# Half of the router's gates added into a DRAM table by indirect DMAs, the other half built by one-hot products at half the density

## Time and profile before

| | |
|---|---|
| runs | 4674.74, 4667.36, 4668.51 us; median 4668.51 |
| span of the profiled execution | 4667.2 us; what lies around the span is not given for it |
| TensorE | 4455.6 us busy, 95% of the span |
| VectorE, ScalarE, GpSimd | 54%, 31%, 7% |
| mean granted clock | 0.981 of 2.4 GHz |
| HBM | 444.94 MB read, 73.40 MB written, 111 GB/s |

### The profile page before, as it was taken

How to read it: one execution, slowest core, us unless ns; L and a number is a source line. 1 busy time by engine, 2 the same in 40 slices (tenths; PEclk the granted TensorE clock), 3 DMA queues, 4 the chain that set the end, 5 groups by cost and what they waited for, 6 DMA issues and landing times. The chain is left out here.

```text
span 4667.2 us, 58760 instructions
## 1 busy us (share of the span) xinstructions
PE 4455.6 (95%) x22068; PEld 3726.6 (80%) x22068; DVE 2500.4 (54%) x3598; ACT 1454.4 (31%) x1579; POOL 306.1 (7%) x178
## 2 busy tenths in 40 slices
PE   8999889999999999989998999899999999999997
PEld 7888658888887778878996887777778888888886
DVE  4333444334335743346777343478888884555554
ACT  3222443222223532223443122233333332222221
POOL 0000000000000000001111000000000001333331
PEclk9999989999999999989999999999999999999998
DMA  3232102223322133222211232345545566565553
GB/s 118 96 90 85 37 29 88 99 88 101 99 89 73 28 91 99 84 72 64 63 59 52 85 98 85 115 131 138 137 128 176 180 193 216 189 198 191 191 193 108
DMA packets 514507, 519.84 MB, mean 111 GB/s; under 512 B 41173, under 2 KB 475469, under 8 KB 513374
## 3 DMA queue, kind: packets, MB, share of 16 engines
q1 hardware_dynamic: 514398, 518.41, 36.4%
HBM read 444.94 MB, written 73.40 MB: 111 GB/s over the span
## 5 line engine op out<-in xcount | busy, mean ns | idle before, releaser
L78 DVE TENSOR_TENSOR w_lo<-w_raw,w_hi 128x2048 fp32r<-128x2048 f32 (+2 forms) x326 | 667.8, 2050 | 919.4 <-ACT w_hi L72 919.3
L72 ACT CAST w_hi<-w_raw 128x2048 fp32r<-128x2048 f32 (+2 forms) x326 | 557.6, 1713 | 1259.1 <-PE psum L3119 491.5
L94 PE MATMUL psum<-h_hi,w_hi 128*128 128x512 f32 x1552 | 612.5, 395 | 16.3 <-DVE w_lo L78 13.3
L96 PE MATMUL psum<-h_hi,w_lo 128*128 128x512 f32 x1552 | 607.6, 391 | 0.0
L95 PE MATMUL psum<-h_lo,w_hi 128*128 128x512 f32 x1552 | 607.5, 391 | 0.0
L94 PE MATMUL psum<-h_hi_peer,w_hi 128*128 128x512 f32 x1104 | 437.6, 396 | 23.9 <-DVE w_lo L2966 16.1
L96 PE MATMUL psum<-h_hi_peer,w_lo 128*128 128x512 f32 x1104 | 431.2, 391 | 0.0
L95 PE MATMUL psum<-h_lo_peer,w_hi 128*128 128x512 f32 x1104 | 430.8, 390 | 0.0
L3117 PE MATMUL psum<-pr_act_hi,w_hi 128*128 128x512 f32 x1024 | 398.3, 389 | 0.0
L3118 PE MATMUL psum<-pr_act_lo,w_hi 128*128 128x512 f32 x1024 | 398.3, 389 | 0.0
L3119 PE MATMUL psum<-pr_act_hi,w_lo 128*128 128x512 f32 x1024 | 398.3, 389 | 0.0
(11 more groups left out here) (467 smaller groups left out, 7432.2 us busy)
## 6 DMA issues: line engine op xcount, KB each, us to landing
w_raw<-in_ffn_w_gate_up_dram SPq DMA_DIRECT2D x176, 512.0 KB, 4.2
w_raw<-in_peer_u_dram SPq DMA_DIRECT2D x256, 256.0 KB, 5.1
w_raw<-in_peer_v_dram SPq DMA_DIRECT2D x128, 512.0 KB, 4.2
w_raw<-in_w_in_dram SPq DMA_DIRECT2D x64, 512.0 KB, 4.3
peer_hidden<-pr_q SPq DMA_DIRECT2D x64, 512.0 KB, 4.0
peer_gates<-pr_staged SPq DMA_DIRECT2D x8, 4096.0 KB, 12.9
pr_back<-peer_hidden SPq DMA_DIRECT2D x64, 512.0 KB, 6.2
pr_gate<-peer_gates SPq DMA_DIRECT2D x64, 512.0 KB, 7.2
```

The source lines that it names most:

```text
L72: c.nc.scalar.copy(c.hi[:, slot, :cols], c.raw[:, slot, :cols]).then_inc(c.hi_ready, 1)
L78: c.nc.vector.tensor_tensor(c.lo[:, slot, :cols], c.raw[:, slot, :cols], c.hi[:, slot, :cols].bitcast(F32), ALU.subtract).then_inc(c.lo_re ...
L94: c.nc.tensor.matmul(out, w_hi, x_hi, start=(n == 0), stop=False)
L96: mm = c.nc.tensor.matmul(out, w_lo, x_hi, start=False, stop=(n == last))
```

## The change

The 512 tokens are split. For tokens 0 to 255 (`ADDED` = 2 blocks of 128) the gates go to a table in DRAM, `gates_added`, with one element for each expert and token, 16.8 MB. The table is cleared in the stick-breaking block by 16 DMAs of 1 MB from a tile of zeros, four behind each group's loads. In `finish`, DVE now also works out where each of the 16 x 2 weights of a token belongs: three more operations, whose result goes to `place`. POOL then issues 32 indirect DMAs a head. Each takes one slot of one block, 128 weights, one from each partition, and adds them in DRAM at the 128 places. Before the next head's DMAs POOL waits until those of the last have landed. SP's first fetch waits for all 256.

For tokens 256 to 511 the one-hot way stays: 64 quads in the same 24 units, 2, 3 and 3 a unit, and four stores of 4 MB. Six transposes of `rows` in place of 12, and copies of half the width. `rows` and `place` now live through the whole layer.

In the output stage `fetch` has three DMAs in place of two (the halves of the gates come from the two tables), POOL's product is two instructions, one for each half of the tokens, and `gated` counts two a unit. The setup makes two more constants on POOL, and PE's first transpose waits for them.

```diff
@@ setup
+            pool.memset(c.zeros[:, :], 0.0).then_inc(made, 1)
+            pool.iota(c.token[:, :], pattern=[[P, 2 * TC]], base=0, channel_multiplier=1,
+                      allow_small_or_imprecise_dtypes=True).then_inc(made, 1)
...
-            pe.wait_ge(made, 13)
+            pe.wait_ge(made, 15)
@@ sb_attention
+GATE_CLEARS = 16
+        cleared = c.gates.rearrange("a p t -> (a p t)").rearrange("(n p x u) -> n p x u", n=GATE_CLEARS, p=P, u=P)
...
                 for j in range(2):
                     load_tile(c, sp, uq + i, j, wide_parts(c, j, w_in, i * 256 + j * D))
+                for q in range(GATE_CLEARS // SB_GROUPS):
+                    part = cleared[bass.ds(i * (GATE_CLEARS // SB_GROUPS) + q, 1)].rearrange("n p x u -> p (n x) u")
+                    sp.dma_start(part, c.zeros[:, :].unsqueeze(1).broadcast_to(list(part.shape))
+                                 ).then_inc(c.gates_cleared, 16)
             following(sp)
+            sp.wait_ge(c.gates_cleared, ROWS_LOADED + 16 * GATE_CLEARS)
@@ peer
+ADDED = 2
+SPREAD = TC - ADDED
-N_TG = T // TG
+N_TG = SPREAD * P // TG
+PICKS = ADDED * TOP
...
-SPREAD_ROUNDS, ROUND_UNITS = 4, 6
+SPREAD_ROUNDS, ROUND_UNITS = 2, 12
-QUADS = ((2, 3), (2, 3), (3, 3)) * 2
+QUADS = ((1, 1), (1, 2), (1, 2)) * 4
...
-                sp.wait_ge(gated, m + 1)
+                sp.wait_ge(gated, m * 2 + 2)
...
+                sp.dma_start(gate_added[:, j], c.gates[bass.ds(m * 2, 2)].rearrange("a p t -> p a t")
+                             ).then_inc(gate_loaded[j], 16)
...
                         sp.wait_ge(written[p], 16 * SPREAD_ROUNDS * ROUND_GROUPS // 2 + 16)
+                    sp.wait_ge(scattered, 16 * NH * PICKS)
...
-            pool.sem_inc(gated, 2)
+            pool.wait_ge(c.gates_cleared, ROWS_LOADED + 16 * GATE_CLEARS)
+            for n in range(NH):
+                pool.wait_ge(placed, n + 1)
+                if n:
+                    pool.wait_ge(scattered, 16 * n * PICKS)
+                for t in range(ADDED):
+                    for k in range(n * TOP, (n + 1) * TOP):
+                        pool.indirect_dma_start(
+                            out=table, out_offset=bass.IndirectOffsetOnAxis(ap=place[:, t, k:k + 1], axis=0),
+                            in_=rows[:, 2, t, k:k + 1], in_offset=None, compute_op=ALU.add).then_inc(scattered, 16)
+            pool.sem_inc(gated, 4)
...
-                    pool.tensor_tensor(prod[:, j].rearrange("p a (g t) -> p a g t", g=N_TG),
-                                       back[:, j].rearrange("p a (g t) -> p a g t", g=N_TG),
+                    some, rest_of = slice(0, ADDED * P), slice(ADDED * P, T)
+                    pool.tensor_tensor(prod[:, j, :, some], back[:, j, :, some], gate_added[:, j], ALU.mult
+                                       ).then_inc(gated, 1)
+                    pool.tensor_tensor(prod[:, j, :, rest_of].rearrange("p a (g t) -> p a g t", g=N_TG),
+                                       back[:, j, :, rest_of].rearrange("p a (g t) -> p a g t", g=N_TG),
                                        gate[:, j].rearrange("p g a t -> p a g t"), ALU.mult).then_inc(gated, 1)
...
+                step(V.scalar_tensor_tensor(spot[:, :, :], rows[:, 0, 0:ADDED, of_head], float(KEYS),
+                                            rows[:, 1, 0:ADDED, of_head], ALU.mult, ALU.add))
+                step(V.scalar_tensor_tensor(spot[:, :, :], spot[:, :, :], float(ADDED * P),
+                                            c.token[:, 0:ADDED].unsqueeze(2).broadcast_to([P, ADDED, TOP]), ALU.mult, ALU.add))
+                V.tensor_copy(place[:, :, of_head], spot[:, :, :]).then_inc(placed, 1)
...
-                for t in range(TC):
-                    mm = nc.tensor.transpose(ps[:, 6 + r % 2, t * P:(t + 1) * P], rows[:, r, t, :], c.ident[:, :])
+                for t in range(SPREAD):
+                    mm = nc.tensor.transpose(ps[:, 6 + r % 2, t * P:(t + 1) * P], rows[:, r, ADDED + t, :],
+                                             c.ident[:, :])
```

More of the change, by code:

```diff
@@ L175, in setup @@
         loaded = c.rows_loaded = [sem(c, f"rows_loaded{t}") for t in range(TC)]
+        c.gates_cleared = c.rows_loaded[3]
         ps = c.psum
@@ L2544 @@
 ROWS_LOADED = 16
+KEYS_LOADED = 16 * (NH // 2)
 BAND = 32
@@ L2584, in peer @@
         q = sb("q", [P, 2, 2, T])
-        chosen = sb("chosen", [P, 3, T])
+        chosen = sb("chosen", [P, 3, SPREAD * P])
+        rows = sb("rows", [P, 3, TC, SLOTS])
+        place = sb("place", [P, ADDED, SLOTS], U32)
         with ExitStack() as pre_ph:
@@ L2604, in peer @@
             total = sb("total", [P, 8], on=pre_ph)
-            rows = sb("rows", [P, 3, TC, SLOTS], on=pre_ph)
+            spot = sb("spot", [P, ADDED, TOP], on=pre_ph)
         with ExitStack() as spread_ph:
@@ L2612, in peer @@
         back = sb("back", [P, 2, 2, T])
+        gate_added = sb("gate_added", [P, 2, 2, ADDED * P])
         gate = sb("gate", [P, 2, N_TG, 2, TG])
         prod = sb("prod", [P, 2, 2, T])
-        keys_loaded, stored, written, hid_loaded, gate_loaded = (
-            [sem(c, f"pr_{n}{j}") for j in range(2)] for n in (
-                "keys_loaded", "stored", "written", "hid_loaded", "gate_loaded"))
+        keys_loaded, stored, written, hid_loaded = (
+            [sem(c, f"pr_{n}{j}") for j in range(2)] for n in ("keys_loaded", "stored", "written", "hid_loaded"))
+        gate_loaded = keys_loaded
         h_free = sem(c, "pr_h_free")
@@ L2620, in peer @@
         (q_taken, keys_turned, keys_taken, scored, s_taken, indexed, steps, shifted, weighed, rows_turned,
-         chosen_taken, turned, gelued, built, spread, taken, gated, hi_done, lo_done, added) = (
+         chosen_taken, turned, gelued, built, spread, taken, gated, hi_done, lo_done, added, placed, scattered) = (
              sem(c, f"pr_{n}") for n in (
@@ L2624, in peer @@
                  "shifted", "weighed", "rows_turned", "chosen_taken", "turned", "gelued", "built", "spread", "taken",
-                 "gated", "hi_done", "lo_done", "added"))
+                 "gated", "hi_done", "lo_done", "added", "placed", "scattered"))
+        table = c.gates.rearrange("a p t -> (a p t)").unsqueeze(1)
         ps = c.psum
@@ L2774, in take_chosen @@
                 act.wait_ge(rows_turned, r + 1)
-                nc.scalar.copy(chosen[:, r, :], ps[:, 6 + r % 2, :]).then_inc(chosen_taken, 1)
+                nc.scalar.copy(chosen[:, r, :], ps[:, 6 + r % 2, 0:SPREAD * P]).then_inc(chosen_taken, 1)
             def stage(o, quads):
@@ L2788, in high @@
             def high(m, j):
-                act.wait_ge(gated, m + 3)
+                act.wait_ge(gated, m * 2 + 6)
                 nc.scalar.copy(act_hi[:, j], prod[:, j]).then_inc(hi_done, 1)
@@ L2845, in _ @@
                     pool.wait_ge(hid_loaded[j], i * 16 + 16)
-                    pool.wait_ge(gate_loaded[j], i * 16 + 16)
+                    pool.wait_ge(gate_loaded[j], i * 32 + (KEYS_LOADED + 32))
                     pool.wait_ge(lo_done, m + 1)
-                    pool.tensor_tensor(prod[:, j].rearrange("p a (g t) -> p a g t", g=N_TG),
-                                       back[:, j].rearrange("p a (g t) -> p a g t", g=N_TG),
+                    some, rest_of = slice(0, ADDED * P), slice(ADDED * P, T)
[3 more added lines that the diff above has]
+                                       back[:, j, :, rest_of].rearrange("p a (g t) -> p a g t", g=N_TG),
                                        gate[:, j].rearrange("p g a t -> p a g t"), ALU.mult).then_inc(gated, 1)
@@ L2899, in finish @@
                 step(V.reciprocal(total[:, 0:TC], total[:, 0:TC]))
-                step(V.tensor_tensor(rows[:, 2, :, n * TOP:(n + 1) * TOP], weight[:, :, :],
+                of_head = slice(n * TOP, (n + 1) * TOP)
+                step(V.tensor_tensor(rows[:, 2, :, of_head], weight[:, :, :],
                                      total[:, 0:TC].unsqueeze(2).broadcast_to([P, TC, TOP]), ALU.mult))
+                step(V.scalar_tensor_tensor(spot[:, :, :], rows[:, 0, 0:ADDED, of_head], float(KEYS),
[3 more added lines that the diff above has]
+                V.tensor_copy(place[:, :, of_head], spot[:, :, :]).then_inc(placed, 1)
             def bests(half, src):
@@ L3188, in count_of_steps @@
 def count_of_steps():
-    a_head = 5 + 1 + 2 + 3 + 3 + 3 + 3
+    a_head = 5 + 1 + 2 + 3 + 3 + 3 + 3 + 2
     return NH * a_head
@@ L3343, in build @@
         c.iota = sb("iota", [P, P])
+        c.zeros = sb("zeros", [P, P])
+        c.token = sb("token", [P, 2 * TC])
         c.vec = sb("vec", [P, P])
@@ L3349, in build @@
         c.begun = sem(c, "begun")
+        c.gates = nc.dram_tensor("gates_added", [KEYS, P, ADDED * P], F32).ap()
         c.hi_ready, c.lo_ready, c.tile_used = (sem(c, n) for n in ("hi_ready", "lo_ready", "tile_used"))
```

## The result

The changed kernel takes 4696.57 us (median of 4 runs, 4695.94 to 4700.19) against 4669.35 for the kernel before (4 runs, 4667.36 to 4674.74). The ratio is 1.006, with a 95% interval of 1.0046 to 1.0074: slower by 27 us, where 4613 was predicted. The profiled execution took 4700.19, with a span of 4698.4.

A forecast was written before the change was run, and what follows sets the result against it. PE, busy for 95% of the span, was taken as the bound. −62 − 0.8 + 4.5 + 1 + 2 = −55.3 from the span of 4667.2 gave 4611.9, so 4613 with 1.3 around the span; range 4603 to 4655, chance 0.8.

The forecast's parts named there:

- Clears, setup, output stage: nothing: Stick-breaking block, setup constants and output stage: clears, two constants, split products and extra fetch are covered, costing 0 us.
- rival A: SP's wait before the first fetch: POOL's scatters come late, gain gone at 3.2 us a DMA; near 4748 at 3.5; chance 0.13.
- rival B: Search stage: POOL's instructions hold DVE up where PE waits for it; +32 us at 0.6 each, near 4645; chance 0.17.
- rival C: Spread stage: builds or copies set the pace, so PE's saving is not had; about 4655 us; chance 0.03.
- The quads, −62: Spread stage: 64 of 128 quads leave PE at 0.953 us each; −61.0 by pace, held 57 to 64, taken as 62.
- The six transposes: Turning of `rows` on PE for two blocks of tokens instead of four: six fewer transposes save 0.8 us.
- DVE's three steps, +4.5: Search stage, in `finish`: two multiply-adds and a cast at 0.25 us each, 0.75 a head, six heads; 0 to 6.
- 5 to 8: Sign to look for: the search stage longer by 5 to 8 us, with the stall after a `finish` about 1.9.
- The adds, 1.5 us each: POOL's 256 indirect DMAs: 1.5 us each, drains about 2 each, ending before 3600, so the chain costs nothing.
- rival A's last paragraph: DVE's fast one-input copies block POOL's descriptors: 3.1 us a DMA, 256 make 794 us, some 20 past the deadline.
- the deadline of 777: From the first head's readiness at 3070.5 to SP's first fetch at 3847: 777 us for POOL's DMAs and drains.
- Contention, +3: Search stage: 1 us for tiny packets on the DMA engines, 2 us for POOL holding DVE up (bounds 0 to 35).

The follow-up runs named there:

- experiment 1: The kernel before with the two new tiles, `zeros` and `token` (544 bytes), allocated at the same place but unused: 4754.96 us, ratio 1.0185.
- experiment 3: The kernel before with the tile `rows` 32 bytes longer, all later tiles 32 bytes further: 4756.02 us, ratio 1.0185.
- experiment 5: The changed kernel with `rows` shortened by 32 bytes, so later tiles move by 512 bytes and not 544: 4611.51 us, ratio 0.9881.
- experiment 2: The changed kernel with `zeros` and `token` taken out of the unused lead, so they push no other tile: 4609.26 us, ratio 0.9875 to the kernel before.
- experiment 12: experiment 2 with three blocks of tokens added instead of two (384 indirect DMAs, 32 quads): 4652.76 us, ratio 0.9967 to the kernel before.
- experiment 11: experiment 2 without POOL's 256 indirect DMAs, those tokens' gates staying zero: 4608.19 us, ratio 0.9872 to the kernel before.

## Why the prediction was wrong

**The step that failed** is the one that opens "Clears, setup, output stage: nothing", in its sentence on the setup: "Two more small constants on POOL precede PE's first transpose, but PE waits for x until 8.24 anyway". I priced the two constants by the time that it takes to fill them, and that is nothing indeed. I didn't price the space that they take. `token`, 32 bytes a partition, cost 87 us (experiments 1, 3 and 5), more than the whole change could win. None of my rivals, A, B or C, has it.

What spoke for it was in sight. The groups by form had 512-column matmuls at 389 to 391 ns and those on `mix_h`, of the same shape, at 396 to 399. `build` has a tile `lead` that nothing uses and a `rows` of 512 − 2 × `TC` numbers, an odd size for rows. I had read neither as a question of speed.

From the step, about 14,700 matmuls of 512 columns that were at the lower level × 0.0067 would be 98 us. Measured were 87. In experiment 3 PE is busy for 4547.0 us, 91.4 more than before, and idle for 207.8 instead of 211.6: a slower PE waits 3.8 us less for others. The remaining 7 us stay open; perhaps not all of the 14,700 run back to back.

**The other steps** are held against experiment 2, which has the work of the change and the distances of before. It was 4609.3 where the sum gave 4613.

- *The quads, −62: right.* The pace gave 61.0, and I took one more. The 24th spread unit's GELU is at 3810.68 and the first quad at 3489.9: 320.8 us, where 321 was named. That is 383.1 − 320.8 = 62.3 less. A quad left over costs (320.8 − 261.1) / 64 = 0.933 us. DVE and the copies didn't pace the stage (rival C): PE was busy in 319.75 of 321 us, and DVE in 213.24. The six transposes that are left cost 0.7 less than the twelve, where 0.8 was named.
- *The products of the quads are still what was read:* 512 records, as predicted.

```profile
L3144 PE MATMUL psum<-pr_first,pr_second 128*128 128x128 f32 x512 | 65.0, 275 | 4.2 <-DVE pr_first L3022 2.9 <-issue 1.3
```

- *DVE's three steps, +4.5: somewhat too high.* The two multiply-adds take 0.19 us each and the cast 0.30, and they start 0.23 us apart. The order of time around one `finish`, and PE's start behind it:

```profile
3238.09 0.19 DVE L2938 SCALAR_TENSOR_TENSOR pr_spot<-pr_rows 128x32 f32<-128x32 f32 x1
3238.32 0.19 DVE L2940 SCALAR_TENSOR_TENSOR pr_spot<-pr_spot,token 128x32 f32<-128x32 f32 x1
3238.55 0.30 DVE L2942 CAST pr_place<-pr_spot 128x32 uint32<-128x32 f32 x1
...
3241.39 2.34 DVE L3007 TENSOR_TENSOR w_lo<-w_raw,w_hi 128x1024 fp32r<-128x1024 f32 x2
...
3243.86 0.49 PE L94 MATMUL psum<-h_hi_peer,w_hi 128*128 128x512 f32 x1 [1.69 <-DVE w_lo L3007]
```

  The stall went from 1.14 to 1.69, where 1.9 was named: five such are +2.8, and a sixth, at the start of the stage, went from 0.92 to 1.25. Over the whole search stage PE is busy 348.37 of 368 us instead of 351.46, 3.1 less. The prediction named 5 to 8 as its sign.
- *The adds, 1.5 us each: too low, and it didn't matter.* One takes 1.54 us in the median and there are 0.3 between two, so the pace is 1.85. But 62 of the 256 take longer than 1.7, up to 4.45, and within a head the mean distance of two is 2.0 to 2.4. The waits for the landings of a head's adds were priced at 2 us each and took 5.0, 35.2 over seven:

```profile
L2869 POOL DMA_INDIRECT gates_added<-pr_rows,pr_place x256: 1537/1545/4452, 3071.2 to 3655.7; - x128
```

  The last is issued at 3655.7, not before 3600, and SP's first fetch, at 3845.02, is still 190 us away. With all waits it is 2.28 us an add, where 777 / 256 = 3.04 would have reached the deadline, so rival A doesn't hold here. Its mechanism is real, as experiment 12 shows at half as many DMAs again. Of the 62 long adds 49 overlap DVE's low part at L3007, a subtraction with two SBUF inputs; of the 194 others 22 do. So it is mostly not the one-input copies of rival A's last paragraph that the long ones stand beside; that the subtraction holds POOL is a reading of the times, not a test. (That paragraph's 794 us also leave out the eight drains that the deadline of 777 has to cover too.)

  The Trainium skill, *DMA: Bandwidth & Descriptors*, "Anatomy of one DMA — SWDGE (gpsimd) path", gives 2.0 us for a DMA from POOL, mostly completion. Here a new one starts every 1.85 us without waiting for the one before, and behind a head's last add POOL stood idle for 5.0 us in the mean until the head's adds had landed. So the nearness of 1.85 to 2.0 says nothing: completion took longer, and it wasn't what set the pace. What POOL does in its 1.54 us no run shows.
- *Contention, +3: none that shows.* Without the adds PE is busy for as long in the search stage (experiment 11). DVE's low part at L3007 takes 1.22 us beside them, as at L2966 before, so rival B doesn't hold. In the output stage of the changed kernel POOL's two products take 2394 and 2447 ns and DVE's low part 2233 instead of 3279. PE had hardly a wait there, before (703.29 of 710 us) and in experiment 2 (702.25), and nothing came of it.
- *Clears and output stage, 0: right.* Four clears hold SP for 10.6 us in one group of the stick-breaking block of the changed kernel. The loads behind them come later, and the first of these holds SP too, for 3.6 us:

```profile
428.53 10.55 SPq L947 DMA_DIRECT2D gates_added<-zeros  x4
439.73 11.25 SPq L65 DMA_DIRECT2D w_raw<-in_sb_w_in_dram  x4
```

  ACT takes those loads 45 us after the first is issued, at 484.79. In experiment 2 the mixer starts at 2058.6, where it started at 2059.6 before: the whole front of the program lost nothing.

The sum with what was measured: −62.3 for the quads, −0.7 for the transposes and +3.1 for DVE's steps are −59.9; experiment 2 gives −59.7. With the +86.0 of the layout by experiment 1, where the work of the change is absent, that makes +26.1 for the changed kernel, where +27.2 was measured.

**Still open:** why 64 bytes cost a third of what 32 do, why two pairs at the same distance modulo 512 bytes differ there, and what the distances between were like. 16 and 256 bytes weren't tried, and both operands were moved together by 32 bytes only. Nor do the runs show which part of the chip the two operands meet in, or why the groups on `mix_h` are slow in the kernel before.

## What to carry to other kernels

And when two groups of the same shape and engine have two durations in one trace, ask what sets the level before you cost a change: it is a lever, or a trap. When a change that should act in one stage moves the start of all later ones, count the matmuls in a full stretch far from it, with the granted clock beside them; that separated a slower step from a wait in one reading.

## What the hardware showed

- A 512-column float32r matmul steps at 0.2267 to 0.2333 us at a granted clock of 1.00, depending on the distance in SBUF between its stationary and its moving operand. With the activations further from the weights than in the kernel before (4669 us): 32 bytes +87 us, 64 +28, 128 +74, 512 nothing, 544 +86. 32 bytes nearer: +91. Both moved by 32 together: nothing. At 64 bytes the distance modulo 512 doesn't settle it: the same `act_hi` takes 392 ns with `w_hi` and 388 with `w_lo`.
- The 264-column matmuls of L95 kept their 284 ns at 544 bytes more, those of L96 went from 284 to 286.
- An indirect DMA from POOL that adds 128 single numbers in DRAM takes POOL 1.54 us in the median, with 1.85 from one to the next; a quarter take longer, up to 4.45, mostly beside a two-input subtraction on DVE. 256 of them beside a nearly full PE and a busy DVE cost nothing that the runs can tell (4608.2 us without, 4609.3 with).
- Four 1 MB stores in a row that read one small tile many times over hold SP for 10.55 us, and the first plain load behind them for 3.6, where such a load takes it 0.45 otherwise. Whether the repeated source, the size or the number of pieces does this, no run tells.
